# Gate spreading in a PEER layer: one comparison for both one-hots and one in-place product with the gates

## What is computed

```python
q = (xn @ w_q).reshape(bsz, t, P_HEADS, 2, P_QDIM // 2)
s = jnp.einsum('bthcd,ckd->bthck', q, sub_keys).astype(jnp.float32)
sv, si = lax.top_k(s, P_TOPK)
...
eid = jnp.take_along_axis(cand_id, top_pos, axis=-1)
gate = jax.nn.softmax(top_s, axis=-1).astype(xn.dtype)
...
hid = jnp.einsum('td,ted->te', xb, u_tab[eb])
return jnp.einsum('te,ted->td', jax.nn.gelu(hid, approximate=False) * gb, v_tab[eb])
```

## Time and profile before

| | us |
|---|---|
| median of three runs | 2783.09 |
| lowest and highest run | 2782.01, 2789.23 |
| span of the profiled execution | 2788.4 |
| `spread_gates` in it, first DVE to last PE work | about 311 (1166.5 to 1477.2) |

### The profile page before, as it was taken

One profiled execution on the slowest core, in us unless ns is written; L12 is line 12 of the kernel. 1 busy time (PEld: TensorE's weight loads), 2 busy tenths in 40 slices (PEclk: granted clock), 3 DMA queues, 4 the chain that ended last, 5 costly groups with the idle time before them and its releaser, 6 DMA issues. The chain is left out here.

```text
span 2788.4 us, 48059 instructions
## 1 busy us (share of the span) xinstructions
PE 2591.0 (93%) x18990; PEld 2521.3 (90%) x18990; DVE 1592.3 (57%) x3204; ACT 855.1 (31%) x1401; POOL 646.3 (23%) x312
## 2 busy tenths in 40 slices
PE   7978998997898989888888999999999999999997
PEld 6976888786898989888888999999999999999997
DVE  4335335343378686599994545545545444677774
ACT  3335234322232323333333222222222222222221
POOL 2423134222245444311112212112122121000000
PEclk9988788775999999999999999999999999999999
DMA  4330000002132333255556323233223232445551
GB/s 178 119 114 22 24 1 23 13 1 80 64 97 87 94 93 100 80 168 167 168 174 232 118 100 124 91 109 109 95 105 110 99 120 75 155 167 178 169 180 48
DMA packets 162451, 296.11 MB, mean 106 GB/s; under 512 B 11872, under 2 KB 99232, under 8 KB 158120
## 3 DMA queue, kind: packets, MB, share of 16 engines
q1 hardware_dynamic: 162344, 294.61, 32.3%
HBM read 230.26 MB, written 64.31 MB: 106 GB/s over the span
## 5 line engine op out<-in xcount | busy, mean ns | idle before, releaser
L114 PE MATMUL banks<-w_high,v_low 128*128 128x288 f32 x2048 | 604.5, 295 | 0.0
L112 PE MATMUL banks<-w_high,v_high 128*128 128x288 f32 x2048 | 603.7, 295 | 0.4
L113 PE MATMUL banks<-w_low,v_high 128*128 128x288 f32 x2048 | 603.0, 294 | 0.0
L112 PE MATMUL banks<-res_hi,u_high 128*128 128x288 f32 x1440 | 433.1, 301 | 10.2 <-ACTq L1966 10.2
L113 PE MATMUL banks<-res_lo,u_high 128*128 128x288 f32 x1440 | 429.4, 298 | 0.0
L114 PE MATMUL banks<-res_hi,u_low 128*128 128x288 f32 x1440 | 429.3, 298 | 0.0
L112 PEld LDWEIGHTS banks<-w_high,v_high 128*128 128x128 f32 x2048 | 384.1, 188 | 3.7 <-DVE w_low L1936 3.7
L114 PEld LDWEIGHTS banks<-w_high,v_low 128*128 128x128 f32 x2048 | 384.2, 188 | 0.0
L113 PEld LDWEIGHTS banks<-w_low,v_high 128*128 128x128 f32 x2048 | 384.1, 188 | 0.0
L1960 DVE TENSOR_TENSOR res_x<-banks,res_x 128x288 f32<-128x288 f32 x512 | 225.0, 454 | 267.2 <-PE banks L114 267.2
L1604 POOL TENSOR_TENSOR u_low<-u_raw,u_high 128x1024 fp32r<-128x1024 f32 x72 | 183.7, 2552 | 710.6 <-ACT u_high L1600 710.6
(11 more groups left out here) (324 smaller groups left out, 4534.6 us busy)
## 6 DMA issues: line engine op xcount, KB each, us to landing
v_raw<-arg_v SPq DMA_DIRECT2D x128, 512.0 KB, 3.9
scratch_gates<-gate_stage SPq DMA_DIRECT2D x18, 2048.0 KB, 9.0
u_raw<-arg_u SPq DMA_DIRECT2D x36, 1024.0 KB, 6.1
gates_in<-scratch_gates SPq DMA_DIRECT2D x32, 1152.0 KB, 7.3
q_raw<-arg_u SPq DMA_DIRECT2D x38, 512.0 KB, 3.6
scratch_hidden<-gelu_ahead SPq DMA_DIRECT2D x56, 288.0 KB, 2.2
gelu_out<-scratch_hidden SPq DMA_DIRECT2D x56, 288.0 KB, 2.8
in_raw<-arg_w_in SPq DMA_DIRECT2D x25, 512.0 KB, 3.9
```

What stands on the lines that cost most here:

```text
L112: pe.matmul(out, ah, bh, start=first, stop=False)
L113: pe.matmul(out, ah, bl, start=False, stop=False)
L114: return pe.matmul(out, al, bh, start=False, stop=last)
```

## The change

The two tiles of one-hots become one, `onehot_pairs`, with a plane 0 (first key) and a plane 1 (second key). One comparison of 128x1024 fills both planes for four tokens. DVE then waits for that comparison by a semaphore (`onehots`), and multiplies plane 1 in place by the four tokens' gates, 128x512, with the gates broadcast along the columns. A new semaphore `gated` tells PE. The number of slots, the matmuls, ACT's, POOL's and SP's lists are unchanged.

```diff
-        onea = core.sb("onehot_first", [P, SLOTS * FOUR, N_KEYS], ctx=ctx)
-        oneb = core.sb("gated_second", [P, SLOTS * FOUR, N_KEYS], ctx=ctx)
+        pair = core.sb("onehot_pairs", [P, SLOTS, 2, FOUR, N_KEYS], ctx=ctx)
...
-                        pe.wait_ge(onehots, it * PER + g + 2)
+                        pe.wait_ge(gated, it * PER + g + 2)
...
-                            ins = pe.matmul(core.psum[:, g % BANKS, t * P:(t + 1) * P], onea[:, s, :], oneb[:, s, :],
-                                            start=True, stop=True)
+                            ins = pe.matmul(core.psum[:, g % BANKS, t * P:(t + 1) * P], pair[:, g % SLOTS, 0, t, :],
+                                            pair[:, g % SLOTS, 1, t, :], start=True, stop=True)
...
                         dve.wait_ge(bank_done, it * PER + g + 1)
-                        s0, k0 = (g % SLOTS) * FOUR, g * FOUR
-                        dve.tensor_tensor(onea[:, s0:s0 + FOUR, :], bc(iota[:, :], 1, [P, FOUR, N_KEYS]),
-                                          bc(cur[:, 0, k0:k0 + FOUR], 2, [P, FOUR, N_KEYS]), ALU.is_equal)
-                        for t in range(FOUR):
-                            s, k = s0 + t, k0 + t
-                            ins = dve.tensor_scalar(oneb[:, s, :], iota[:, :], cur[:, 1, k:k + 1], cur[:, 2, k:k + 1],
-                                                    ALU.is_equal, ALU.mult)
-                        ins.then_inc(onehots, 1)
+                        dve.tensor_tensor(pair[:, g % SLOTS],
+                                          iota[:, :].unsqueeze(1).unsqueeze(1).broadcast_to([P, 2, FOUR, N_KEYS]),
+                                          bc(cur[:, 0:2, g * FOUR:(g + 1) * FOUR], 3, [P, 2, FOUR, N_KEYS]),
+                                          ALU.is_equal).then_inc(onehots, 1)
+                        dve.wait_ge(onehots, it * PER + g + 1)
+                        o = pair[:, g % SLOTS, 1]
+                        dve.tensor_tensor(o, o, bc(cur[:, 2, g * FOUR:(g + 1) * FOUR], 2, [P, FOUR, N_KEYS]),
+                                          ALU.mult).then_inc(gated, 1)
```

More of the change, by code:

```diff
@@ L1617, in spread_gates @@
         cur = core.sb("cur_picks", [P, 3, 2 * TB], ctx=ctx)
-        onea = core.sb("onehot_first", [P, SLOTS * FOUR, N_KEYS], ctx=ctx)
-        oneb = core.sb("gated_second", [P, SLOTS * FOUR, N_KEYS], ctx=ctx)
+        pair = core.sb("onehot_pairs", [P, SLOTS, 2, FOUR, N_KEYS], ctx=ctx)
         stage = core.sb("gate_stage", [P, 2, NG, TB, JJ], ctx=ctx)
         onehots = core.sem("onehots_ready")
+        gated = core.sem("seconds_gated")
         bank_done = core.sem("gates_done")
@@ L1695, in _ @@
                     for g in range(PER):
-                        pe.wait_ge(onehots, it * PER + g + 2)
+                        pe.wait_ge(gated, it * PER + g + 2)
                         pe.wait_ge(staged, it * PER + g + 1)
                         for t in range(FOUR):
-                            s = (g % SLOTS) * FOUR + t
-                            ins = pe.matmul(core.psum[:, g % BANKS, t * P:(t + 1) * P], onea[:, s, :], oneb[:, s, :],
-                                            start=True, stop=True)
+                            ins = pe.matmul(core.psum[:, g % BANKS, t * P:(t + 1) * P], pair[:, g % SLOTS, 0, t, :],
+                                            pair[:, g % SLOTS, 1, t, :], start=True, stop=True)
                         ins.then_inc(bank_done, 1)
@@ L1746, in _ @@
             def _(dve):
-                dve.sem_inc(onehots, 1)
+                dve.sem_inc(gated, 1)
                 dve.sem_inc(bank_done, SLOTS)
                 with dve.Fori(0, steps) as it:
-                    dve.wait_ge(onehots, it * PER + 1)
+                    dve.wait_ge(gated, it * PER + 1)
                     dve.tensor_copy(cur[:, :, :], sel[:, :, bass.ds(it * (2 * TB), 2 * TB)]).then_inc(copied, 1)
```

## The result

The changed kernel takes 2796.65 us (median of six runs, 2788.87 to 2799.95), the kernel before beside it 2786.16 (six runs, 2782.01 to 2790.41). The ratio is **1.0036, 95% interval 1.0022 to 1.0051**: 10 us slower. The interval leaves out 1, and it has in it the 0.3% at which the prediction parts "same" from "slower". The profiled execution has a span of 2797.9 us, 9.5 above the 2788.4 of before.

A forecast was written before the change was run, and what follows sets the result against it. Neither DVE nor PE alone was taken as the bound: they alternate, four slots apart. Terms 5.1 + 2.5 + 1.1 - 1.5 = +7.2 us on the median 2783.1 gave 2790 us, range 2781 to 2800.

The forecast's parts named there:

- A group from 1.63 to 1.86: DVE's time per group, start to start: 0.23 us more, times 144 groups, +33.1 us of DVE work.
- POOL: 4.2 lost a step: DVE's group beside POOL's two subtractions loses 4.2 us a step instead of 4.08: +1.1 us over nine steps.
- Slack of 28.0: DVE's 34 waits for PE, with lost overlap, absorb 28.0 of the 33.1 us added, leaving +5.1 us.
- Waits that stay, 2.5: DVE's slack for PE is not all usable: +2.5 us, bounds 0 and 5.
- The end of the stage, -1.5: After DVE's last group, less work is queued at PE: up to 3.3 us won, taken as -1.5.
- (1): Group beside POOL: subtractions run unbroken, DVE's lead never fills; +14 us, 2797; chance 0.23 together with (5).
- (2): PE's clock: one more stretch at 1.2 GHz a step, half absorbed; +15 us, 2798; chance 0.11.
- (3): Beside POOL's subtractions, DVE's new instructions meet no contention; -30 us, 2753; chance 0.03.
- (4): DVE's group costs its summed durations, 2.04 us before and 1.90 after; -20 us, 2763; chance 0.03.
- (5): DVE's comparison: broadcast over three dimensions costs extra columns' time, raising the time; chance 0.23 together with (1).

The follow-up runs named there:

- the waits experiment: Kernel before with a semaphore wait between each two of a group's four TENSOR_SCALAR, three waits a group; ratio 1.0086 (1.0058 to 1.0115).

## Why the prediction was right, and where its sizes were off

The mechanism was the forecast's: 2790 us in a range of 2781 to 2800, measured 2796.65. Of the 6.6 us between them, 3.1 are not the change's: the median of before is 2786.16 over six runs and was 2783.09 over the three that the forecast started from. The change itself was put at 7.2 us and measures 10.5 by medians and 9.4 by stage. Step by step:

- *A group from 1.63 to 1.86.* Exact: comparison 1.218 (1.220 worked out), gap 0.03, product 0.69 and next start 0.61 after it. The method that carried it was to take starts, not durations: by durations the five instructions were 2.04 us and the change a gain. The waits between the four TENSOR_SCALARs, and the 31 us between the two eight-slot kernels, show it.
- *POOL: 4.2 lost a step.* Measured 4.19 in the steps where the pair begins on a comparison. In the first, fifth and ninth the pair begins on a product, and 4.2 is spread over two groups:

```profile
1312.87 1.22 DVE L1754 TENSOR_TENSOR onehot_pairs<-numbers,cur_picks 128x1024 f32<-128x1024 f32 x1
1314.12 2.76 DVE L1760 TENSOR_TENSOR onehot_pairs<-onehot_pairs,cur_picks 128x512 f32<-128x512 f32 x1
1316.81 3.37 DVE L1754 TENSOR_TENSOR onehot_pairs<-numbers,cur_picks 128x1024 f32<-128x1024 f32 x1
...
1328.93 1.23 DVE L1754 TENSOR_TENSOR onehot_pairs<-numbers,cur_picks 128x1024 f32<-128x1024 f32 x1 [0.58 <-PE banks L1699]
```

- *Slack of 28.0.* A little less. A step with no wait is 34.57 to 34.58 (the third, fourth, seventh and eighth of the changed kernel); against before's mean of 33.76 over eight steps and its settled 34.13 in the ninth that is 0.81 x 8 + 0.44 = 6.9 us, where my work less slack and POOL's term gave 5.1 + 1.1 = 6.2.
- *Waits that stay, 2.5.* Measured 3.0, read as what groups take over 1.86: about 0.1 to 1.0 in the first, second, fifth, sixth and ninth step.
- *The end of the stage, -1.5.* This is the term that was off most: 9.4 - 6.9 - 3.0 leaves -0.5. Read directly it is -0.7: PE's last group starts 4.8 us after DVE's last product ends (1480.35 to 1485.17), where it was 5.5 before. I had less work queued up at PE there; but the ninth step is one of those in which PE was behind and DVE had to wait. With eight slots, where DVE waits in neither kernel, it is 5.2 us against 7.9, so the end is shorter by 2.7 and the mechanism exists, in another case.

```profile
1479.66 0.69 DVE L1760 TENSOR_TENSOR onehot_pairs<-onehot_pairs,cur_picks 128x512 f32<-128x512 f32 x1
...
1485.17 0.99 PEld L1699 LDWEIGHTS banks<-onehot_pairs 128*128 128x128 f32 x8
```

Terms as measured: 6.9 + 3.0 - 0.5 = 9.4 against my 7.2. These two microseconds lie on either side of the 8.3 at which the prediction parts "same" from "slower"; with errors of this size in the small terms, which side the time falls on is chance.

The rivals. (1), POOL's pair unbroken: not seen, the DVE instruction got in between in all nine steps. (2), PE's clock: seen in part. Read in stretches of 1 us, the granted clock of the kernel before is at 0.50, 1.2 GHz, for some 6.8 us in eight of its nine steps; the 3.4 us of the prediction are those of the second step, the only short one. In the changed kernel it is 3.4 us in the fourth step, 6.8 in five, and 10.2 in the first, fifth and ninth. In the fifth, PE had two stops of 2.77 and 1.94 us in place of one long one (stretches; columns as in the earlier trace rows):

```profile
1314.00:1317.00 3.00, 0.23 (x3) 0.06 (x1) 2.97 (x3) 1.83 (x3) 3.00 (x2) 0.94 1.04 290
1317.00:1320.00 3.00, 2.02 (x8) 1.72 (x8) 3.00 (x1) 0.60 (x1) 2.10 (x1) 0.50 0.89 249
1320.00:1323.00 3.00, 2.04 (x9) 2.05 (x10) 2.93 (x5) 0.00 (x0) 0.00 (x0) 0.50 0.00 0
1323.00:1327.00 4.00, 4.00 (x19) 4.00 (x18) 3.93 (x5) 0.60 (x1) 0.00 (x0) 0.51 0.00 0
1327.00:1330.00 3.00, 3.00 (x28) 3.00 (x27) 2.39 (x3) 1.19 (x3) 0.00 (x0) 1.00 0.00 0
```

PE then is late enough that DVE waits again (0.58 at 1328.93). The slow clock and the residual waits come together in the trace: all but one of the seven waits are in these three steps. With eight slots two steps have 10.2 us at the slow clock, and DVE waits for PE in none. That one causes the other was not tried apart. (3) is out: DVE does stand still. (4), durations add up, is out by the waits experiment. (5): 1218 ns for the broadcast over three dimensions is the plain price.

## What to carry to other kernels

Price a VectorE instruction by the distance between starts, not by its duration: the short independent ones here overlap by 0.08 us, and a fused form that makes the second half depend on the first gives the overlap back and adds columns (1.63 us a group became 1.86). A hand-over with few slots hides added work until its slack is used up, so before judging a change by its time, ask how much of it is in waits of the engine that grew; the same edit cost 9 us of stage with four slots and 31 with eight. And when an engine stands still beside another that reads two operands from SBUF, moving that work onto the engine that it blocks can be cheaper than the block (here 31 us of stage less, with 2.3 us more of DVE work a step).

## What the hardware did that I had not expected

POOL's two-operand subtraction can be kept out while DVE issues two-operand instructions without a gap: 17.6 us for 2.35 us of work, with DVE's instructions at ordinary length meanwhile, until DVE had to wait. It isn't always so. In the same kernel POOL got in at once where its record starts 0.07 to 0.08 us before a comparison, and was kept out where it starts 0.20 to 0.28 us after the start of one. The changed kernel has a gap of 0.03 us behind every comparison, through the very wait that costs it time, and there POOL got in at the next gap in all five cases in which its record starts early in a comparison. How the chip chooses between the two engines is open.

The Trainium skill, "SBUF — State Buffer", section "Who interferes with whom", says that a VectorE instruction with two SBUF inputs contends with a GpSimd instruction that reads SBUF, and, of VectorE's two-port modes, that whoever issues first gets the shared pair for the whole instruction and the other blocks. The trace agrees for one instruction against one (3.38 us for a 1.22 us comparison), but shows that among a run of them the one that waits isn't always next in turn. Once in, POOL does keep DVE out for its whole length.
